# Two schedule entries moved in a fused two-block transformer kernel: linear attention's squares ahead of the third gate, its last two transposes behind one piece

## The chip, the cores and the metric

The kernel runs on one core of a Trainium2 chip. The metric is device time in microseconds (us) for one launch. TensorE does the matrix products, VectorE and ScalarE the elementwise work and the copies out of PSUM, GpSimd one subtraction per piece of weights, SyncE only starts DMAs.

## The reference, cut to what matters

Two layers of a first transformer block are followed by two layers of a second one; batch 1, 256 tokens, width 1024, float32. The change lies in the second block. Its mixer has three branches that are gated, added and projected:

```python
o_nsa = nsa_attention(...)                       # branch 0
o_gla = gated_linear_attention(...)              # branch 1
o_mem = memory_attention(...)                    # branch 2
gates = jax.nn.sigmoid(merge.reshape(B, S, 3, D) + b_merge)
merged = (gates[:, :, 0] * (o_nsa @ w_branch[0]) + gates[:, :, 1] * (o_gla @ w_branch[1])
          + gates[:, :, 2] * (o_mem @ w_branch[2]))
x = x + merged @ w_out
# the end of gated_linear_attention:
o = rms_norm(o, norm_g).reshape(B, S, H * GLA_HEAD_DV)
return o * jax.nn.silu(r)
```

The normalisation of `o` needs, for each token and each of 4 heads, the sum of 128 squares. That is the work whose place is changed, with the transposes that bring the finished branch into the layout that TensorE wants.

## The kernel before, in words

All weights pass through the core once, as 616 pieces of 128 x 1024 floats. SyncE loads a piece into a ring of seven slots (`raw`); ScalarE rounds it to the matmul's format (`round_piece`, L1275, tile `hi`, a ring of five); GpSimd subtracts the rounded part (L542, tile `lo`, in four quarters within the mixers); TensorE multiplies by both parts (L569 to L571, three matmuls for one product: hi by hi, hi by lo, lo by hi) and raises `used`, which frees the slots. ScalarE rounds four pieces ahead (`AHEAD`): the step of a piece on ScalarE rounds the piece four places later in the stream, and needs the `hi` slot that the piece five places before that one has freed.

The order within a mixer is written out by hand. `mix2_work()` says which steps stand behind each piece; `mix2_order()` turns this into one list, and each engine's program walks that list and issues its own part of every step. So an engine's order is fixed, and a step's wait holds up all that the engine has behind it.

At the end of the mixer the order is the four pieces of the memory branch, `rows (2,0)` to `(2,3)`; the four of the NSA branch, `rows (0,0)` to `(0,3)`; two of the linear attention branch, `(1,0)` and `(1,1)`; then `last_branch`, with that branch's other two and the eight of `w_out`. In `last_branch` TensorE takes the first token tile of several pieces before the second tile of any of them. Between them stand:

- `gate b` (ScalarE only, L1631): two sigmoids, 128 x 1024 each. They come behind `(2,0)`, `(2,1)` and `(2,2)`, for branches 2, 0 and 1; `exp_and_ln()` behind the last of them loads the table set of exp and ln (L1264).
- `branch b, m` (VectorE only, L2272 and L2278 or L2282): the product of a branch with its gate, read from PSUM. `rows (0,0)` writes the same banks as the memory branch's, so TensorE waits there for `branch 2, 0` and, before the second token tile, for `branch 2, 1`.
- `gla[3]`: ScalarE waits for `og` (VectorE's copy L2138, the last output of linear attention) and squares eight blocks of 128 columns with a running sum (L1534); VectorE multiplies by the silu of `r` (L2092).
- `gla[4]`: VectorE waits for the sums and takes the variance (L1729). `gla[5]`: ScalarE's `Ln` and `Exp` (L1281, L1282), VectorE's four small steps (L1720 to L1723) and the scaling (L2098), which raises `gscaled`.
- `gla[6]` and `gla[7]`: TensorE waits for `gscaled` and transposes four blocks (L1035) into one bank each; ScalarE takes the rounded part out (`high_part`, L1422, raises `y2hi`), VectorE the rest (L2104, raises `y2lo`). `rows (1,0)` waits for the banks and for `y2lo`.
- `nsa_unit` and `gla_unit`: the last steps of the two attentions, behind `(2,0)` and `(2,1)`.

Of the kernel before, what the change touches and what calls it, by code (L numbers as in the profile page):

```python
# [116 lines left out]
def mix2_work():  # L117

    windows, prep, mem, memory_in, gla, nsa = (
        [(name, i) for i in range(9)] for name in ("windows", "prep", "mem", "memory_in", "gla", "nsa"))  # L120
    cmp = [("cmp", k // 4, k % 4) for k in range(8)]
    mu = [("mem_unit", t) for t in range(6)]
    gu = [[("gla_unit", hp, t) for t in range(5)] for hp in range(2)]
    decay = [[("decay", hp, i) for i in range(4)] for hp in range(2)]
    nu = [("nsa_unit", t) for t in range(NSA_UNITS + 2)]
    none = ()
    return {
        "nk": (none, none, none, none),
        "nq": (none, [memory_in[0]], none, [memory_in[1]]),
        "z3": ([prep[0], windows[0]], [memory_in[2]], [prep[1], windows[1]], [prep[2]]),  # L130
        "mk": (none, [prep[3]], none, [cmp[0], mem[0]]),
        "mq": ([cmp[1], mem[1]], [cmp[2], mem[2]], [cmp[3], mem[3]], [cmp[4], mem[4]]),
        "mv": ([mem[8], cmp[5], mem[5]], [cmp[6], mem[6]], [cmp[7], ("take_cmp",), mem[7]], [mu[0]]),
        "gqk": ([mu[1]], [nsa[0], mu[2]], [mu[3], nsa[1]], [nsa[6], nsa[2]]),
        "gv": ([mu[4], nsa[3]], [gla[0]], [mu[5], nsa[4]], [gla[1], nsa[5]]),
        ("merge", 0): ([gla[2], nu[0]], [decay[0][0]], [nu[1], decay[0][1]], none),
        ("merge", 1): ([nu[2], decay[0][2]], [nu[3]], [decay[0][3]], [nu[4]]),
        ("merge", 2): ([gu[0][0]], [nu[5]], [gu[0][1]], [nu[6], gu[0][2]]),
        ("merge", 3): ([gu[0][3]], [nu[7]], [gu[0][4], decay[1][0]], [nu[8], decay[1][1]]),
        ("merge", 4): ([nu[9], decay[1][2]], [nu[10]], [nu[11], decay[1][3]], [nu[12]]),  # L140
        ("merge", 5): ([gu[1][0]], [nu[13]], [gu[1][1]], [nu[14]]),
        "gr": ([gu[1][2]], [nu[15]], [gu[1][3]], [nu[16]]),
        ("rows", 2): ([nu[17]], [nu[18], gu[1][4]], [gla[3], gla[4]], [gla[5]]),
        ("rows", 0): (none, [gla[6]], [gla[7]], none),
        ("rows", 1): (none, none),
    }


def mix2_order():
    order, merges, work = [], 0, mix2_work()  # L150
    for i, name in enumerate(STRIPS2):
        behind = work[(name, merges) if name == "merge" else name]
        merges += name == "merge"
        for j in range(4):
            order.append(("strip", i, j))
            if j == 3:
                order.append(("take", i))
            order += behind[j]
    for b in BRANCHES:
        for i, steps in enumerate(work["rows", b]):  # L160
            order.append(("rows", b, i))
            if b == 2 and i < 3:
                order.append(("gate", BRANCHES[i]))
            if i == 3:
                order += [("branch", b, m) for m in range(MT)]
            order += steps
    order.append(("last_branch",))
    return order
# [2423 lines left out]
```

## Time and profile before

| | us |
|---|---|
| median of 3 runs (lowest to highest) | 1975.81 (1975.54 to 1976.88) |
| the profiled execution | 1974.96 |
| its span, first to last instruction | 1972.9 |

| engine | busy us | share of the span | instructions |
|---|---|---|---|
| TensorE matmuls (PE) | 1951.8 | 99% | 9698 |
| TensorE weight loads (PEld) | 1578.3 | 80% | 9698 |
| VectorE (DVE) | 719.3 | 36% | 1686 |
| ScalarE (ACT) | 1041.4 | 53% | 1746 |
| GpSimd (POOL) | 1592.1 | 81% | 1160 |

The mean granted clock of TensorE is 0.998 of full speed. The DMA queues moved 348.6 MB, 177 GB/s on average. A share of busy time is an average over stages; what an edit is worth is read where it stands. The second block's two layers have the edited stretch at about 1240 to 1290 us and at 1720 to 1770 us of the span. In the views below, times are microseconds from the start of the span; brackets behind a row give the engine's idle time just before it and what ended it; x4 means four instructions merged into the row.

### The profile page before, as it was taken

Reading aid. Unit: us, or ns where it says so; the run is one execution under the profiler, and the core shown is the slowest. Engines: PE = TensorE matmul, PEld = TensorE weight load, DVE = VectorE, ACT = ScalarE, POOL = GpSimd, SP = SyncE. Lnnn points to the kernel's source line nnn. Section 1 sums busy time; section 2 is a strip of 40 time slices with the busy share of each in tenths; the row PEclk is TensorE's granted clock in tenths of the full one; section 3 lists DMA queues with packets and bytes.
Section 4 is the critical chain, followed back from the end, with each engine's and each line's share of the span. In section 5 each row is a group of like instructions: output and inputs, shape, how many; then the busy total and the mean of one; then the engine's idle time right before and its main releaser. Section 6 shows DMA issues by size and latency. Waiting matters only on the chain.

```text
span 1972.9 us, 26543 instructions
## 1 busy us (share of the span) xinstructions
PE 1951.8 (99%) x9698; PEld 1578.3 (80%) x9698; DVE 719.3 (36%) x1686; ACT 1041.4 (53%) x1746; POOL 1592.1 (81%) x1160
## 2 busy tenths in 40 slices
PE   9999999999999999999999999999999999999999
PEld 7888777888888877788887877778888777778887
DVE  4534444100300354500035677521114577642111
ACT  6445666444644466644466444654446554555443
POOL 7988776988788877598879687878887968788885
PEclk9999999999999999999999999999999999999999
DMA  6655434555565543456565333456557433345553
GB/s 239 233 208 171 161 118 158 184 192 188 206 221 186 178 164 125 139 206 249 186 225 191 119 138 125 153 174 217 211 185 260 150 127 120 129 143 188 183 190 128
DMA packets 98204, 348.63 MB, mean 177 GB/s; under 512 B 13436, under 2 KB 14108, under 8 KB 97820
## 3 DMA queue, kind: packets, MB, share of 16 engines
q1 hardware_dynamic: 97372, 345.80, 49.8%
q8 instruction: 78, 1.28, 0.3%
q10 hardware_dynamic: 704, 1.14, 0.2%
q14 instruction: 50, 0.41, 0.1%
HBM read 345.85 MB, written 1.05 MB: 176 GB/s over the span
## 4 chain that ended last, share of the span: by engine, by line
PE 94%; POOL 2%; ACT 2%; DVE 1%; issue 0%; DMA 0%; SPq 0%; POOLq 0%; ACTq 0%; DVEq 0%
PE psum L569 28%; PE psum L571 27%; PE psum L570 27%; POOL lo L542 2%; PE psum L709 2%; PE psum L752 1%; PE psum L639 1%; PE psum L775 1%; PE psum L762 1%; PE psum L985 1%; PE psum L742 1%; ACT big L1631 1%; ACT hi L1275 0%; PE psum L1139 0%; PE psum L798 0%; PE psum L839 0%
## 5 line engine op out<-in xcount | busy, mean ns | idle before, releaser
L542 POOL TENSOR_TENSOR lo<-raw,hi 128x256 fp32r<-128x256 f32 (+1 forms) x1156 | 1591.9, 1399 | 366.6 <-ACT hi L1275 338.4
L1275 ACT ACTIVATE hi<-raw 128x1024 fp32r<-128x1024 f32 x616 | 646.7, 1059 | 510.7 <-PE psum L571 489.7
L569 PE MATMUL psum<-hi,h_hi 128*128 128x512 f32 x1632 | 651.5, 399 | 2.5 <-POOL lo L542 2.2
L571 PE MATMUL psum<-hi,h_lo 128*128 128x512 f32 x1632 | 637.7, 391 | 0.0
L570 PE MATMUL psum<-lo,h_hi 128*128 128x512 f32 x1632 | 636.5, 390 | 0.0
L569 PEld LDWEIGHTS psum<-hi,h_hi 128*128 128x128 f32 x1632 | 307.3, 188 | 72.4 <-POOL lo L542 6.1
L571 PEld LDWEIGHTS psum<-hi,h_lo 128*128 128x128 f32 x1632 | 306.4, 188 | 65.8
L570 PEld LDWEIGHTS psum<-lo,h_hi 128*128 128x128 f32 x1632 | 307.0, 188 | 60.0
L569 PE MATMUL psum<-hi,y_hi 128*128 128x512 f32 x832 | 333.9, 401 | 4.0 <-DVE big L2272 4.0
L1814 DVE SCALAR_TENSOR_TENSOR big<-psum,small,big 128x256 f32<-128x256 f32 (+1 forms) x120 | 61.1, 551 | 750.4 <-ACT big L1368 750.4
L571 PE MATMUL psum<-hi,y_lo 128*128 128x512 f32 x832 | 325.6, 391 | 0.0
L570 PE MATMUL psum<-lo,y_hi 128*128 128x512 f32 x832 | 325.0, 391 | 0.0
L569 PEld LDWEIGHTS psum<-hi,y_hi 128*128 128x128 f32 x832 | 156.6, 188 | 38.7 <-DVE big L2272 4.9
L571 PEld LDWEIGHTS psum<-hi,y_lo 128*128 128x128 f32 x832 | 156.6, 188 | 33.9
L570 PEld LDWEIGHTS psum<-lo,y_hi 128*128 128x128 f32 x832 | 157.0, 189 | 30.2
L1417 ACT ACTIVATE soft<-soft,small 128x128 f32<-128x128 f32 (+1 forms) x120 | 54.6, 456 | 121.0 <-DVE small L1850 98.3
L1368 ACT ACTIVATE big<-psum,small 128x256 f32<-128x256 f32 (+1 forms) x120 | 57.1, 527 | 83.8 <-PE psum L571 83.7
L1822 DVE TENSOR_TENSOR y_lo<-psum,y_hi 128x512 fp32r<-128x512 f32 (+1 forms) x60 | 49.4, 824 | 38.3 <-ACT y_hi L1377 38.3
L1748 DVE SCALAR_TENSOR_TENSOR h_lo<-psum,special,h_hi 128x128 fp32r<-128x128 f32 x160 | 44.1, 344 | 42.0 <-ACT h_hi L1292 42.0
L1292 ACT ACTIVATE h_hi<-psum,special 128x128 fp32r<-128x128 f32 x160 | 44.5, 379 | 24.6 <-PE psum L639 24.6
L1377 ACT ACTIVATE y_hi<-psum 128x512 fp32r<-128x512 f32 (+1 forms) x60 | 42.8, 713 | 13.1 <-PE psum L709 13.1
L1869 DVE COPY soft<-psum 128x384 f32<-128x384 f32 (+2 forms) x68 | 35.4, 520 | 24.9 <-PE psum L752 24.9
(264 smaller groups left out, 1362.2 us busy)
## 6 DMA issues: line engine op xcount, KB each, us to landing
raw<-in_stream SPq DMA_DIRECT2D x616, 512.0 KB, 3.2
big<-in_w SPq DMA_DIRECT2D x14, 512.0 KB, 7.6
big<-in_post SPq DMA_DIRECT2D x6, 512.0 KB, 4.6
special<-in_b_merge SPq DMA_DIRECT2D x2, 1536.0 KB, 8.1
memkv<-in_mem SPq DMA_DIRECT2D x2, 1024.0 KB, 5.7
big<-in_band SPq DMA_DIRECT2D x2, 768.0 KB, 4.8
x<-in_x SPq DMA_DIRECT2D x2, 512.0 KB, 5.0
special<-in_special SPq DMA_DIRECT2D x2, 512.0 KB, 4.4
```

The costliest lines, as they stand in the source:

```text
L542: t = pool.tensor_tensor(M.lo[:, slot, w], M.raw[:, slot, w], f32(M.hi[:, slot_hi, w]), ALU.subtract)
L569: pe.matmul(out, lhs_hi, rhs_hi, start=start, stop=False)
L570: pe.matmul(out, lhs_hi, rhs_lo, start=False, stop=False)
L571: return pe.matmul(out, lhs_lo, rhs_hi, start=False, stop=stop)
L1275: act.activation(M.hi[:, slot_hi, :], M.raw[:, slot, :], ACT.Copy).then_inc(sem["hi"], 1)
L1292: t = act.activation(out_hi[:, k, toks], psum[:, bank, i * P:i * P + P], ACT.Copy, scale=1.0 if gain is None else gain[:, k:k + 1])
L1368: t = act.activation(act_s[:, m, :], psum[:, bank + m, 0:width], ACT.Silu if gated else ACT.Relu, scale=V.scale[:, m:m + 1])
L1377: act.activation(flat(out), flat(psum[:, bank:bank + kts // 2, :]), ACT.Copy).then_inc(sem["yhi"], 1)
L1417: t = act.activation(out, prob[:, w], ACT.Exp, scale=-1.0, bias=mn[:, i:i + 1], accum_out=total[:, i:i + 1])
L1748: t = dve.scalar_tensor_tensor(out_lo[:, k, toks], psum[:, bank, i * P:i * P + P], gain[:, k:k + 1], f32(out_hi[:, k, toks]), ALU.mult, AL ...
L1814: t = dve.scalar_tensor_tensor(prod_s[:, m, :], psum[:, bank + m, col:col + width], V.scale[:, m:m + 1], act_s[:, m, :], ALU.mult, ALU.mult)
L1822: dve.tensor_tensor(flat(y_lo[:, kt, :]), flat(psum[:, bank:bank + kts // 2, :]), f32(flat(y_hi[:, kt, :])), ALU.subtract).then_inc(sem["y ...
```

## The change

Two steps get another place in the list; nothing is added or taken away, and both layers of the second block have the edit. `gla[3]` moves from behind `rows (2,2)` to behind `rows (2,1)`, and so in front of `gate 1`, the third gate. `gla[6]` moves from behind `rows (0,1)` to behind `rows (0,2)`, where `gla[7]` stands; `(0,2)` is the third piece of the NSA branch (the words that come with the change call it the memory branch's).

```diff
@@ mix2_work()
-        ("rows", 2): ([nu[17]], [nu[18], gu[1][4]], [gla[3], gla[4]], [gla[5]]),
-        ("rows", 0): (none, [gla[6]], [gla[7]], none),
+        ("rows", 2): ([nu[17]], [nu[18], gu[1][4], gla[3]], [gla[4]], [gla[5]]),
+        ("rows", 0): (none, none, [gla[6], gla[7]], none),
         ("rows", 1): (none, none),
```

## Rows read from the trace of the kernel before

**Rows 1.** The page's chain that ended last, shares of the span by engine.

```profile
PE 94%; POOL 2%; ACT 2%; DVE 1%; issue 0%; DMA 0%; SPq 0%; POOLq 0%; ACTq 0%; DVEq 0%
```

**Rows 2.** TensorE's waits: engine line <- releaser: us in total, times, longest.

```profile
PE psum L569 <- DVE big L2272: 4.0, 2, 2.0
...
PE psum L569 <- POOL lo L542: 2.2, 4, 1.3
```

**Rows 3.** Chain of waits, first layer: start us, us, engine and line.

```profile
1247.51 0.36 ACT y_hi L1422
1247.87 0.95 ACT hi L1275
...
1250.74 1.28 ACT L1264
1252.03 0.74 ACT big L1534 x5
...
1254.49 0.95 ACT hi L1275
1255.51 2.84 POOL lo L542 x4
...
1268.37 4.62 POOL lo L542 x4
...
1282.74 3.71 POOL lo L542 x4
```

**Rows 4.** Timeline of VectorE, first layer: start us, us, engine, line, operation, tiles.

```profile
1248.52 0.42 DVE L2138 COPY big<-psum 128x256 f32<-128x256 f32 x1 [0.19 <-PE psum L1002]
...
1254.69 2.35 DVE L2272 TENSOR_TENSOR big<-big,psum 128x1024 f32<-128x1024 f32 x2
...
1259.28 1.72 DVE L2098 TENSOR_TENSOR big<-big,small 128x1024 f32<-128x1024 f32 x1
```

**Rows 5.** Timeline of ScalarE, first layer.

```profile
1255.57 0.21 ACT L1282 ACTIVATE small<-small 128x8 f32<-128x8 f32 x1
...
1262.19 0.69 ACT L1422 ACTIVATE y_hi<-psum,special 128x512 fp32r<-128x512 f32 x1 [2.04 <-PE psum L1035]
```

**Rows 6.** Timeline of TensorE, first layer.

```profile
1252.44 0.39 PE L569 MATMUL psum<-hi,y_hi 128*128 128x512 f32 x1
...
1255.97 0.50 PE L569 MATMUL psum<-hi,y_hi 128*128 128x512 f32 x1 [2.01 <-DVE big L2272]
...
1261.55 0.60 PE L1035 MATMUL psum<-consts,big 128*128 128x128 f32 x4
...
1267.96 0.39 PE L569 MATMUL psum<-hi,y_hi 128*128 128x512 f32 x1
...
1274.76 0.39 PE L569 MATMUL psum<-hi,y_hi 128*128 128x512 f32 x1
...
1286.49 0.50 PE L569 MATMUL psum<-hi,h_hi 128*128 128x512 f32 x1 [1.30 <-POOL lo L542]
```

**Rows 7.** Timeline of TensorE, second layer.

```profile
1735.65 0.73 PE L569 MATMUL psum<-hi,y_hi 128*128 128x512 f32 x1 [2.01 <-DVE big L2272]
...
1739.40 0.39 PE L569 MATMUL psum<-hi,y_hi 128*128 128x512 f32 x1
...
1766.79 0.50 PE L569 MATMUL psum<-hi,h_hi 128*128 128x512 f32 x1 [0.43 <-POOL lo L542]
```

**Rows 8.** Stretch 1736 to 1741: length, busy by engine, then granted clock, DMA share, GB/s.

```profile
1736.00:1741.00 5.00, 5.00 (x16) 3.91 (x16) 4.51 (x6) 1.05 (x2) 4.86 (x6) 0.68 0.06 22
```

**Rows 9.** Timeline of GpSimd, first and second layer.

```profile
1255.51 33.27 POOL L542 TENSOR_TENSOR lo<-raw,hi 128x256 fp32r<-128x256 f32 x37 [2.81 <-ACT hi L1275]
...
1735.19 9.73 POOL L542 TENSOR_TENSOR lo<-raw,hi 128x256 fp32r<-128x256 f32 x12 [2.80 <-ACT hi L1275]
...
1748.39 14.29 POOL L542 TENSOR_TENSOR lo<-raw,hi 128x256 fp32r<-128x256 f32 x16 [0.38 <-ACT hi L1275]
1763.03 6.06 POOL L542 TENSOR_TENSOR lo<-raw,hi 128x256 fp32r<-128x256 f32 x5 [0.35 <-ACT hi L1275]
```

## The prediction

> **What bounds the kernel now.** I read the page's chain first: TensorE holds 94% of it, GpSimd and ScalarE 2% each [rows 1]. So only TensorE's idle time can be won, and there is little of it. The list of its waits has two entries that touch the edited stretch [rows 2]: 4.0 us in two waits on VectorE's L2272 (the memory branch times its gate) and 2.2 us in four waits on GpSimd's L542. Then I read the chain of waits around the first wait on L2272 [rows 3]. The reader is to see that it does not run through that wait. It comes down ScalarE (`y_hi`, rounding, sigmoids, table load, squares, rounding), crosses to GpSimd at 1255.51 and stays there for nine pieces, until TensorE goes on at 1286.49. GpSimd's own timeline says the same: 37 quarter pieces in 33.27 us with no idle time inside [rows 9]. A piece costs GpSimd 2.84 us undisturbed [rows 3], and 0.14 to the next; TensorE takes two and a half from 1267.96 to 1274.76 [rows 6], 2.72 each. GpSimd is the slower of the two here, and the lead it had is used up at the end of the nine. I name pieces by branch and number; the nine are (0,3), (1,0), (1,1), the two of `last_branch` (LB0, LB1) and the first four of `w_out` (E0 to E3).
>
> So TensorE's wait of 2.01 us before (0,0) at 1255.97 is visible but covered: it still stands 1.30 us for E3 [rows 6], and would stand longer if it came sooner. In the second layer the same wait of 2.01 is followed by half clock: the granted clock is 0.68 over 1736 to 1741 [rows 8], so TensorE was at 1.2 GHz for part of it, and a matmul takes 0.73 us instead of 0.39 [rows 7]. From 1735.65 to 1739.40 it does three quarters of a piece, 3.75 us for what takes 3 x 0.68 and about 0.1 for the start: 1.6 us lost. There GpSimd has three short waits for ScalarE's rounding (0.38 and 0.35 are two of them [rows 9]), and TensorE still stands 0.43 us for E3 at 1766.79 [rows 7].
>
> **The change, part by part.** No piece changes its place, so the stream, SyncE's DMAs and their queue, and GpSimd's order are as before. On VectorE nothing moves: `gate` and `rows` issue nothing there, so `gla[3]` to `gla[7]` keep their order among its instructions.
>
> (a) `gla[3]` moves ahead of `rows (2,2)` and of the gate of branch 1. On ScalarE the eight squares now come right behind the `y_hi` of `nsa_unit` 18, ahead of the rounding of (0,2), two sigmoids and the table load. They bring a wait that costs nothing now: `og`, set by VectorE's copy L2138, which ends at 1248.52 + 0.42 = 1248.94 [rows 4]; before, ScalarE comes to it at 1252.03, long after [rows 3]. Now it arrives at 1247.87, the end of `y_hi`, and stands 1.1 us; and 0.1 us of overlap is lost, by which the rounding's start ran ahead of that end. Queued behind the wait on ScalarE are the rounding of (0,2), the sigmoids, the load, and the rounding of (0,3), for which GpSimd waits. These and the squares only swap places, so the rounding of (0,3) ends 1.2 us later, and GpSimd starts on it at 1255.51 + 1.2 = 1256.7. The second layer repeats the first up to this point (2.80 us of GpSimd's idle time ahead of the nine against 2.81 [rows 9]): 1735.19 + 1.2 = 1736.4.
>
> (b) What it buys. The squares take 1254.49 - 1252.03 = 2.46 us [rows 3], so their sums are there at about 1251.5. L2272 is then free to start when the first token tile of (2,3) is done, about 1252.6 (the second tile starts at 1252.44 [rows 6], and the first one's last matmul ends some 0.15 later). One takes 1.2 (2.35 for two [rows 4]), so TensorE may go on at 1253.9, where the second tile is done anyway. The 2.0 us wait goes to 0 to 0.2 in each layer, and with it the cause of the half clock. Taken alone: 2.05 in the first layer, 2.05 + 1.6 in the second, 5.7 in all.
>
> (c) What is late next: GpSimd. The nine pieces take it 1282.74 + 3.71 - 1255.51 = 30.94 us, including the time it is blocked beside VectorE's work (4.62 for LB1 against 2.84) [rows 3]. All of these VectorE steps still fall inside the nine, so I keep 30.94. Their rounding comes in time, since TensorE, being earlier, frees the `hi` slots earlier. First layer: the low part of LB1 is ready at 1268.37 + 4.62 + 1.2 = 1274.2, where TensorE now wants it at 1274.76 - 2.05 = 1272.7: a new wait of 1.5, and 0.55 of the lead is left. Without GpSimd it would be at E3 at 1286.49 - 1.30 - 0.55 = 1284.6; the low part is ready at 1286.45 + 1.2 = 1287.65, so 3.0 more in waits before E2 and E3 together. TensorE passes this point at 1287.7 instead of 1286.49, **+1.2 us**. Second layer: 1736.4 + 30.94 = 1767.35 against 1766.79: **+0.6 us**, since GpSimd's old gaps close. Behind the nine GpSimd waits for TensorE again, so the loss neither grows nor is won back.
>
> (d) `gla[6]` moves behind `rows (0,2)`: four transposes, one `y_hi`, one `y_lo`, as many as before. `gscaled` comes at 1259.28 + 1.72 = 1261.0 [rows 4]; the `Exp` L1282 in front of its chain ends at 1255.78 [rows 5], now 1257.0, where VectorE came to need it before too (L2272 ends at 1254.69 + 2.35). TensorE reaches the old place at 1261.55 - 2.05 = 1259.5 [rows 6] and would stand 1.5 there; behind (0,2) it arrives at 1262.2. Who waits for the moved step: (1,0) needs the banks and `y2lo` of both pairs. With transposes until 1263.1 and two `y_hi` of 0.69 [rows 5], each with a `y_lo` of about that length behind it, they are there by 1265.0, and (1,0) starts at 1267.96 - 2.05 = 1265.9. I cost it at nothing; if that cover of 0.9 fails, GpSimd's nine pieces hide up to 1.5. On ScalarE the rounding of LB0 is now ahead of both `y_hi` and that of LB1 behind both, ready about 1265.2; GpSimd wants it at 1268.37 + 1.2. Nothing.
>
> (e) A table load that the trace doesn't show: `Square` now runs between two pairs of sigmoids, and before it stands behind the load of the exp and ln set. The nearest row is the rounding, a `Copy` between the sigmoids with no load [rows 3]. So 0, or two loads of 1.28 each [rows 3] in front of the rounding of (0,3); a load can't be saved, since no other set is left out. I take 0, as for `Copy`.
> On this the Trainium skill, "ScalarE: Activation LUTs", section "Table sets: the hidden batching unit", says that cheap functions (it names relu, copy, identity and abs) are in every set; it does not name square. Its section "What ACT_TABLE_LOAD costs" puts a switch at 2.66 us with its drain; here a load takes 1.28 and the next instruction starts 0.01 later, so the row decides. By the page's figure two would be an estimated 5.3 us per layer in place of 2.6.
>
> Sum: +1.2 + 0.6 = +1.8 us. The profiled execution took 1974.96 (its span of 1972.9 and 2.1 around it) and would be 1976.8. It lay 0.85 below the median of the runs, 1975.81; on that the forecast is **1977.6**.
>
> **The rivals.**
> *A, the wait was the loss.* GpSimd keeps up and TensorE keeps the 5.7 us: 1970.1. For it: these two waits are the largest in the list [rows 2]. Against: the nine pieces without idle time [rows 9]. It decides by the start of the nine: they would have to begin some 2 us before 1255.5, not after, or take under 28 us.
> *B, table loads.* Two more put the rounding of (0,3) 1.2 + 2.6 = 3.8 us late: +3.8 and +3.2, 1982.8. It decides by whether the sigmoid's set has `Square`.
> *C, the clock, ending slower.* Waits of 1.5 and twice about 1.5 within 14 us take the place of one of 2.0. Of the two waits of 2.01 one was followed by half clock; the one of 1.30 was not. Half clock ahead of E3 costs nothing, since GpSimd sets that point; from E3 on it costs up to 1.6 a layer: 1979.2 with one, 1980.8 with both.
> *D, it doesn't do what it says.* The words that come with the change put the last transposes behind the memory branch's third piece, (2,2); there they would wait for `gscaled` some 10 us. The code puts them behind (0,2), so this has no weight.
>
> **How the numbers follow.** The forecast as in (c): 0.58, 1976.5 to 1978.7. C in one layer 0.14, in both 0.05. A: 0.10. B: 0.08. Faults of the sum (the nine pieces 0.5 shorter or longer in each layer, by how GpSimd's quarters meet VectorE's work; the cover in (d)): 0.05. For 8 in 10 the range holds all but A and B: 1975.0 to 1980.9. A measurement of this kernel tells about 0.2%, 4 us, from no change. Faster by that (below 1971.9) is A and a little of the rest: 0.11. Slower (above 1979.8) is B, C in both layers and a part of C in one: 0.17. Within: 0.72.
>
> **What would show it.** Right: TensorE's waits on L2272 fall from 4.0 to under 0.5 us and those on L542 rise from 2.2 to about 9 to 10, with new ones before LB1 and E2; ScalarE idles 1.1 us before its first square, released by L2138; GpSimd idles before (0,2) and again before (0,3), then works for 31 us without a gap in both layers; the clock stays whole near 1736. Wrong: a rounding of (0,3) that ends before 1255.5; no wait on L542 near 1274; a table load beside L1534 (B); a granted clock under 1 behind E3 (C).

## The result and the profile after

The kernel after takes 1978.42 us (median of 20 runs, 1977.19 to 1979.89) and the kernel before 1975.43 (20 runs, 1974.71 to 1976.88). The ratio is 1.0014 (95%: 1.0008 to 1.0020): 2.8 us slower, 1.6 to 4.0 (the medians are 3.0 apart). The forecast was 1977.6, and 1.8 slower. The profiled executions took 1977.62 and 1974.96, 2.66 apart.

TensorE's waits in the kernel after (engine line <- releaser: us in total, times, longest), against [rows 2]:

```profile
PE psum L569 <- POOL lo L542: 5.3, 5, 2.0
PE psum L1035 <- DVE y_lo L2104: 3.1, 2, 1.6
```

The wait on L2272 is gone from the list. In its place stand 3.1 us more for GpSimd, and an entry that the kernel before does not have at all: the transposes of the linear attention (L1035) wait for VectorE's `y_lo`.

ScalarE's timeline of after, first layer, against [rows 3]:

```profile
1247.42 0.36 ACT L1422 ACTIVATE y_hi<-psum 128x256 fp32r<-128x256 f32 x1
1248.88 0.31 ACT L1534 ACTIVATE big<-big 128x128 f32<-128x128 f32 x1 [1.10 <-DVE big L2138]
...
1251.24 1.05 ACT L1275 ACTIVATE hi<-raw 128x1024 fp32r<-128x1024 f32 x1
1252.19 2.00 ACT L1631 ACTIVATE big<-big 128x1024 f32<-128x1024 f32 x2
1254.20 1.28 ACT L1264 ACT_TABLE_LOAD   x1
1255.50 1.06 ACT L1275 ACTIVATE hi<-raw 128x1024 fp32r<-128x1024 f32 x1
```

The squares come first, after 1.10 us of standing still for the copy L2138. Behind them are the rounding of (0,2), the sigmoids, one table load, and the rounding of (0,3), which ends at 1256.56 where it ended at 1255.44. No load stands beside L1534.

VectorE's timeline of after, first layer, against [rows 4]:

```profile
1252.54 2.58 DVE L2272 TENSOR_TENSOR big<-big,psum 128x1024 f32<-128x1024 f32 x2 [0.93 <-PE psum L571]
```

L2272 now waits for TensorE's products (L571) and no longer for the squares, and starts 2.15 us sooner.

GpSimd's timeline of after, first and second layer, against [rows 9]:

```profile
1252.36 2.84 POOL L542 TENSOR_TENSOR lo<-raw,hi 128x256 fp32r<-128x256 f32 x4 [3.87 <-ACT hi L1275]
1256.64 33.49 POOL L542 TENSOR_TENSOR lo<-raw,hi 128x256 fp32r<-128x256 f32 x37 [1.44 <-ACT hi L1275]
...
1733.97 2.85 POOL L542 TENSOR_TENSOR lo<-raw,hi 128x256 fp32r<-128x256 f32 x4 [3.87 <-ACT hi L1275]
1738.24 33.56 POOL L542 TENSOR_TENSOR lo<-raw,hi 128x256 fp32r<-128x256 f32 x37 [1.43 <-ACT hi L1275]
```

It stands before (0,2), stands again before (0,3), and then works through 37 instructions. These are the 36 quarters of the nine pieces and one whole piece behind them (2.38 us), which the view counts in with the quarters. The nine pieces start 1.1 us later on the clock of the trace (1256.64 against 1255.51), and they set the end.

TensorE's timeline of after, against [rows 6] and [rows 7]:

```profile
1264.29 0.33 PE L1035 MATMUL psum<-consts,big 128*128 128x128 f32 x1 [1.56 <-DVE y_lo L2104]
...
1284.91 0.63 PE L569 MATMUL psum<-hi,h_hi 128*128 128x512 f32 x1 [1.99 <-POOL lo L542]
...
1288.18 0.65 PE L569 MATMUL psum<-hi,h_hi 128*128 128x512 f32 x1
...
1290.17 0.48 PE L569 MATMUL psum<-hi,h_hi 128*128 128x512 f32 x1
...
1766.56 0.50 PE L569 MATMUL psum<-hi,h_hi 128*128 128x512 f32 x1 [2.00 <-POOL lo L542]
...
1769.51 0.50 PE L569 MATMUL psum<-hi,h_hi 128*128 128x512 f32 x1 [0.85 <-POOL lo L542]
```

The waits are before E2 (1.99 and 2.00) and E3. In the first layer TensorE comes to E3 late instead of waiting for it, because half clock follows the wait for E2. Two stretches of after, 1284 to 1289 and 1736 to 1741 (columns as in [rows 8]):

```profile
1284.00:1289.00 5.00, 4.09 (x13) 3.31 (x14) 0.66 (x2) 0.86 (x4) 4.86 (x6) 0.66 0.01 3
1736.00:1741.00 5.00, 5.00 (x23) 4.06 (x22) 3.08 (x5) 4.37 (x6) 3.57 (x6) 1.00 0.64 197
```

So near 1736, where the kernel before had 0.68, the clock is whole. The half clock (1.2 GHz) has gone to the first layer.

The account of the 2.66: TensorE comes to this stretch 0.1 us earlier than in the trace of before. It passes E3's second token tile at 1290.17, against this row of before:

```profile
1288.36 0.48 PE L569 MATMUL psum<-hi,h_hi 128*128 128x512 f32 x1
```

That makes 1.8 + 0.1 = 1.9 lost in the first layer. In the second it passes E3 at 1769.51 against 1766.79, 2.7, of which 1.8 was brought along: 0.9 lost there. Behind E3 the two traces run in step.

### The profile page after: what moved, and what is told of

Same layout as the page of the kernel before. It is cut to its first block, busy times and chain, and to the rows that moved or that the text cites. A ratio compares the mean times of both kernels' runs of the same rounds, so it can differ in the third digit from the quotient of the medians.

```text
span 1975.6 us, 26543 instructions
## 1 busy us (share of the span) xinstructions
PE 1952.4 (99%) x9698; PEld 1578.5 (80%) x9698; DVE 718.8 (36%) x1686; ACT 1043.0 (53%) x1746; POOL 1591.9 (81%) x1160
## 3 DMA queue, kind: packets, MB, share of 16 engines
q8 instruction: 78, 1.28, 0.3%
HBM read 345.85 MB, written 1.05 MB: 176 GB/s over the span
## 4 chain that ended last, share of the span: by engine, by line
PE 94%; POOL 4%; ACT 1%; DVE 0%; issue 0%; DMA 0%; SPq 0%; POOLq 0%; DVEq 0%; ACTq 0%
PE psum L569 28%; PE psum L571 27%; PE psum L570 27%; POOL lo L542 4%; PE psum L709 2%; PE psum L752 1%; PE psum L639 1%; PE psum L762 1%; PE psum L775 1%; PE psum L985 1%; PE psum L742 1%; PE psum L1139 0%; PE psum L839 0%; PE psum L798 0%; PE psum L941 0%; PE psum L953 0%
## 5 line engine op out<-in xcount | busy, mean ns | idle before, releaser
L542 POOL TENSOR_TENSOR lo<-raw,hi 128x256 fp32r<-128x256 f32 (+1 forms) x1156 | 1591.7, 1400 | 369.5 <-ACT hi L1275 340.7
L571 PE MATMUL psum<-hi,h_lo 128*128 128x512 f32 x1632 | 638.2, 391 | 0.0
L571 PEld LDWEIGHTS psum<-hi,h_lo 128*128 128x128 f32 x1632 | 306.7, 188 | 65.6
L571 PE MATMUL psum<-hi,y_lo 128*128 128x512 f32 x832 | 325.0, 391 | 0.0
L571 PEld LDWEIGHTS psum<-hi,y_lo 128*128 128x128 f32 x832 | 156.1, 188 | 33.9
```

What stands on the lines that cost most here:

```text
L542: t = pool.tensor_tensor(M.lo[:, slot, w], M.raw[:, slot, w], f32(M.hi[:, slot_hi, w]), ALU.subtract)
L571: return pe.matmul(out, lhs_lo, rhs_hi, start=False, stop=stop)
```

## The experiments

The theory (T): GpSimd's nine pieces set the end of the stretch, so what counts is when (0,3) is rounded, and the squares ahead of it delay that. The main rival (R): the loss comes from somewhere else, from the new wait of the moved transposes or from the clock. Each kernel was timed in 5 rounds beside the kernel before on the same chip, whose median was 1975.5 to 1975.8 each time. Ratios are to it, with the 95% interval; differences in us come from the ratio or from the medians, which differ by up to 0.6 us. A piece's rounding has the number of its piece, although `round_piece` is called `AHEAD` steps before.

### One half of the change at a time

e1 is the kernel before with `gla[3]` moved alone, e2 with `gla[6]` moved alone.

```diff
-        ("rows", 2): ([nu[17]], [nu[18], gu[1][4]], [gla[3], gla[4]], [gla[5]]),
+        ("rows", 2): ([nu[17]], [nu[18], gu[1][4], gla[3]], [gla[4]], [gla[5]]),
```
```diff
-        ("rows", 0): (none, [gla[6]], [gla[7]], none),
+        ("rows", 0): (none, none, [gla[6], gla[7]], none),
```

> Only the squares move; the two transposes stay where they were. Theory (GpSimd's nine pieces, started by the rounding of (0,3), set the point E3): the rounding is as late as in the changed kernel, so the time is that of the changed kernel, +2.7 us on the kernel before, although TensorE now waits 1.6 us a layer for gscaled in front of the first transposes. Rival (the time is lost in TensorE's new wait at the last transposes, 1.57 us a layer behind (0,2)): that wait is gone, and what comes in its place decides; if waiting for gscaled is as dear the two can't be told apart here.

> Only the first pair of transposes moves, the squares stay behind the third gate. TensorE gets the wait of 1.57 us a layer for the first pair's low part. Theory: GpSimd's nine pieces start and end as before; the wait uses up TensorE's old waits for E3 (1.30 and 0.43 us), so the time is 0.3 + 1.1 = +1.4 us. Rival (the wait at the transposes counts in full): +3.1 us. Rival (only the squares matter): 0.

The squares alone: 1978.85 us, 1.0016 (1.0007 to 1.0025), as slow as both together. The transposes alone: 1978.31, 1.0012 (1.0003 to 1.0021). TensorE's waits of e1, and after them those of e2:

```profile
PE psum L569 <- POOL lo L542: 4.5, 4, 2.0
...
PE psum L1035 <- DVE big L2098: 2.4, 2, 1.2
```
```profile
PE psum L569 <- DVE big L2272: 4.0, 2, 2.0
PE psum L1035 <- DVE y_lo L2104: 3.1, 2, 1.6
```

In e1 the transposes wait 1.2 us for `gscaled` at their old place, and it costs nothing beyond what after has. So the squares alone are enough for the whole loss of the change. In e2 the wait for L2272 stays as it was, and the transposes' wait comes on top. The 2.4 us (0.6 to 4.1) lie between what T and R gave, so the time alone decides nothing between them. The runs of e2 also fall into two groups, five at 1976.0 to 1976.5 and six at 1978.3 and above. The trace says more. GpSimd's timeline of e2, first layer:

```profile
1284.48 6.06 POOL L542 TENSOR_TENSOR lo<-raw,hi 128x256 fp32r<-128x256 f32 x5 [0.36 <-ACT hi L1275]
```

GpSimd has caught up and stands 0.36 us just before E3, for ScalarE's rounding; so GpSimd doesn't set E3 here. With the later start of its trace taken off, TensorE passes E3 0.75 us later than in before in the first layer and 1.7 in the second. In the first layer 0.9 of the 1.57 were covered by the wait for E3 (1.30 before, 0.40 here), in the second nothing was (0.43 in both). T had put 0.3 and 1.1 there. The halves don't add up: 3.1 + 2.4 would be 5.5 where both together cost 2.8.

### Does the moved transposes' wait cost anything in the kernel after?

`gla[7]` waits until both output banks are read out, so behind (0,2) it waits for the `y_lo` of the pair just before it. e6 is the kernel after in which each pair waits for its own bank.

```diff
-                wait_free(0)
-                wait_free(1)
+                wait_free(pair)
```

> The changed kernel, in which the second pair of last transposes waits for its own bank alone and no longer for the first pair's. TensorE's wait of 1.57 us a layer there goes. Theory: GpSimd still sets E2 and E3, its nine pieces start as late, so the time stays within 0.5 us of the changed kernel (+2.3 to +3 on the kernel before) and TensorE's waits for GpSimd grow by the 3.1 us. Rival (the wait at the transposes is what the change costs): 3.1 us less than the changed kernel, -0.3 on the kernel before.

1978.2 us, 1.0013 (1.0004 to 1.0021): as the kernel after. TensorE's waits of e6, and then its timeline, first layer:

```profile
PE psum L569 <- POOL lo L542: 6.9, 6, 2.0
```
```profile
1274.47 0.51 PE L569 MATMUL psum<-hi,y_hi 128*128 128x512 f32 x1 [1.23 <-POOL lo L542]
```

The entry on L1035 is gone, and the time is given back further down: a wait of 1.23 us before LB1 appears, the one that the prediction had priced at 1.5. R falls: the 1.57 us a layer are idle time that GpSimd hides.

### Is it the date of (0,3)'s rounding?

e3 keeps the squares ahead of the gate, but rounds (0,2) before them and (0,3) before the sigmoids.

```diff
             elif i == 3:
+                round_piece(piece["rows", 2, 2] + AHEAD)
                 act.wait_ge(sem["og"], 4 * layer + 4)
...
             elif what == "gate":
                 b = step[1]
+                if b == 1:
+                    round_piece(piece["rows", 2, 3] + AHEAD)
```

> The changed kernel, with ScalarE's rounding of (0,2) put ahead of its wait for og and the rounding of (0,3) put right behind the squares, ahead of the third gate. Nothing else moves. Theory: GpSimd starts the nine pieces at 1252.7 instead of 1256.6, E3's low part is there by 1283.9, and TensorE comes at 1284.9 with its waits for the memory branch's product and the half clock gone: -1.6 in the first layer, -2.1 in the second, -3.7 us on the kernel before, 6.4 below the changed kernel. Rival (the new wait at the transposes or the clock is what the change costs): within 1 us of the changed kernel, +1.7 to +3.7.

1972.32 us, 0.9984 (0.9975 to 0.9992): 3.2 faster than before and 6 faster than after, with the squares where the change put them. GpSimd's timeline of e3, first layer (its trace runs 1.6 us later than that of before at this point; over 8 to 16 us, at the start of the kernel, its granted clock is 0.57 and that of before 0.79):

```profile
1250.52 6.78 POOL L542 TENSOR_TENSOR lo<-raw,hi 128x256 fp32r<-128x256 f32 x8 [0.29 <-ACT hi L1275]
1258.72 24.03 POOL L542 TENSOR_TENSOR lo<-raw,hi 128x256 fp32r<-128x256 f32 x28 [1.41 <-ACT hi L1275]
```

(0,2) and (0,3) now follow each other without idle time. The gap of 1.41 is before (1,0), whose rounding has become the late one.

e4b turns the same knob the other way: the kernel before, with four unused copies on ScalarE in front of the rounding of (0,3).

```diff
             elif what == "rows":
+                if step == ("rows", 2, 3):
+                    for _ in range(4):
+                        own(act.activation(V.gla_prod[:, 1024:1280], M.x[:, 0, 0:256], ACT.Copy))
                 round_piece(piece[step] + AHEAD)
```

> The kernel before, with four extra ScalarE copies of 128 x 256 (results not used, about 1.7 us together) in front of the rounding of (0,3); the squares and TensorE's waits up to (0,0) are untouched. Theory: GpSimd's nine pieces start 1.7 us later, +1.7 in the first layer and +1.1 to +1.7 in the second: about +3 us, all of it in TensorE's waits for GpSimd near E2 and E3, with the two waits of 2.0 for the memory branch's product as before. Rival (that product's wait is what bounds this stretch): 0.

1979.68 us, 1.0018 (1.0009 to 1.0027): 3.6 slower. Timeline of e4b, ScalarE and then GpSimd, and its waits of TensorE:

```profile
1254.83 1.74 ACT L1626 ACTIVATE big<-x 128x256 f32<-128x256 f32 x4
1256.60 1.06 ACT L1275 ACTIVATE hi<-raw 128x1024 fp32r<-128x1024 f32 x1
```
```profile
1257.74 33.46 POOL L542 TENSOR_TENSOR lo<-raw,hi 128x256 fp32r<-128x256 f32 x37 [4.59 <-ACT hi L1275]
```
```profile
PE psum L569 <- POOL lo L542: 6.1, 6, 2.0
PE psum L569 <- DVE big L2275: 4.0, 2, 2.0
```

The copies take 1.74 us. The wait for the memory branch's product (here L2275) is untouched, and the waits for GpSimd rise from 2.2 to 6.1. A delay of the rounding, without any squares, makes the loss. The granted clock is whole in both layers behind the waits of 2.0 (1.00 over 1285 to 1290 and over 1767 to 1772), and that execution took 1978.63, 3.7 more than the profiled one of before; so half clock isn't needed for the loss. (An earlier form with two copies of 128 x 1024 has a race between the copies and the squares and gave no time.)

### Is an early rounding enough without the squares?

e10 is the kernel before with (0,3) rounded right behind the sigmoids, ahead of the table load and of the squares.

```diff
                 if b == 1:
+                    round_piece(piece["rows", 2, 3] + AHEAD)
+                if b == 1:
                     exp_and_ln()
```

> The kernel before with one edit: the rounding of (0,3) right behind the third gate's sigmoids, ahead of the table load and the squares; squares and transposes as in the kernel before. GpSimd starts the nine pieces 3 us sooner, but the squares end 1.3 us later (0.3 for the slot of (2,2), 1.0 for the rounding), and with them VectorE's product and (0,0). Theory: TensorE's wait at (0,0) grows from 2.0 to 3.3, its waits for GpSimd at E3 (1.30 and 0.43) go, and what bounds is TensorE: -0.05 in the first layer, +0.9 in the second, 0 to +1 in all, more if half clock follows the longer waits. Rival (GpSimd alone counts): -1.7 or better.

1979.42 us, 1.0019 (1.0010 to 1.0028): 3.8 slower, a miss for both. The squares now end later, and L2272 with them. TensorE's waits of e10 (L2274 is L2272 there):

```profile
PE psum L569 <- DVE big L2274: 7.4, 2, 3.7
```

3.7 us a layer, and half clock behind it in both layers. GpSimd's timeline of e10, first layer:

```profile
1286.00 6.06 POOL L542 TENSOR_TENSOR lo<-raw,hi 128x256 fp32r<-128x256 f32 x5 [0.35 <-ACT hi L1275]
```

Here too GpSimd stands 0.35 us before E3, in both layers, and TensorE's own pace sets the end. Counted from where each trace comes to the wait for L2272, TensorE passes E3 2.3 us later than in before in the first layer and 1.7 in the second, 4.0 in all. The 1.7 are the longer wait in full (3.68 against 2.01); the half clock stood in that layer of before as well. In the first layer the half clock is new too, and 0.9 of both is covered (the wait for E3 was 1.30 and is 0.43). So GpSimd covers the wait for L2272 only as long as it is itself the later one. Squares first and roundings first are both needed; either alone loses.

### Both together: a version that beats both kernels

e8 is e3 with the pair's own bank (the edit of e6) and with (1,0) rounded ahead of the table load too.

```diff
                 if b == 1:
+                    round_piece(piece["rows", 0, 0] + AHEAD)
+                if b == 1:
                     exp_and_ln()
```

> e3_round_first with two more edits: the rounding of (1,0) stands behind the third gate's sigmoids, ahead of the table load, and the second pair of last transposes waits for its own bank alone. In e3_round_first GpSimd stood idle 1.4 us between (0,3) and (1,0), still ended last at E3 (waits of 0.5 and 0.4 us), and TensorE lost 1.57 us a layer at the transposes. Theory: E3 is ready 1.3 us sooner and TensorE is there 1.6 sooner: 1.2 to 1.6 us less in each layer than e3_round_first, -5.7 us on the kernel before. Rival (something else than GpSimd's pieces sets the pace): no better than e3_round_first, -3.3.

1970.12 us, 0.9971 (0.9960 to 0.9982): 5.4 faster than the kernel before by the medians and 8.3 faster than the kernel after. GpSimd's timeline of e8 and then its waits of TensorE:

```profile
1249.18 37.48 POOL L542 TENSOR_TENSOR lo<-raw,hi 128x256 fp32r<-128x256 f32 x41 [0.31 <-ACT hi L1274]
```
```profile
PE psum L569 <- POOL lo L542: 2.5, 4, 1.1
```

One run from (0,2) on, the 40 quarters of ten pieces and one whole piece; neither of the two gaps is left. What remains of waiting is about 1.05 for E3 in each layer. (e8 has 7 runs, 1969.88 to 1970.56.)

e5 leaves (1,0)'s rounding out of e8, and e11 leaves the own bank out of it.

> e8_three_rounded without its early rounding of (1,0): the roundings of (0,2) and (0,3) early, and the second pair of transposes waiting for its own bank alone. Theory: TensorE comes to E3 1.57 us sooner than in e3_round_first, but GpSimd's pieces from (1,0) on start as late as there, and e3_round_first waited for them already; so the time is that of e3_round_first (-3.4 on the kernel before) within 0.6 us. Rival (the transposes' wait is what is left): 3.1 us less, -6.5.

> e8_three_rounded with TensorE's wait for the first pair's low part put back. In e8_three_rounded TensorE stood 1.0 us for E3 in each layer, and the wait put back is 1.57. Theory: the first 1.0 of it is covered, so 0.5 to 0.6 us a layer slower than e8_three_rounded, -4.4 on the kernel before. Rival (each wait counts in full): 3.1 slower than e8_three_rounded, -2.4.

e5: 1972.36 us, 0.9983 (0.9974 to 0.9992), as e3: the rounding of (1,0) is worth 2.2. e11: 1972.32, 0.9985 (0.9976 to 0.9994), 2.2 slower than e8, between what the two theories gave. The chain of waits of e11, first layer, shows what E3 waits for there (its start, with L639, is as in the chain of before that stands further down):

```profile
1280.33 0.46 ACT h_hi L1292 x2
1280.79 0.95 ACT hi L1275
1281.81 3.73 POOL lo L542 x4
1285.58 0.50 PE psum L569
```

GpSimd is idle for 0.36 us before E3, since E3's rounding stands on ScalarE behind the `h_hi` of TensorE's own transposes (L639). From the transposes to E3 it is a loop of TensorE itself, and whatever delays TensorE ahead of it delays the end one for one. So the idle time that GpSimd hid in after and e6 (1.57 us a layer) costs here, since GpSimd is no longer late: 2.2 of 3.1. The theory had covered 1.0 a layer by e8's wait for E3; but 0.43 of such a wait is part of the loop, and counted from the copy that sets `og`, E3 comes 1.2 us later in e11 in the first layer and 1.1 in the second.

### Whole pieces for E0 to E3

A whole piece takes GpSimd 2.40 us, four quarters take 2.84 and 0.14 to the next piece. e7b is the kernel after with E0 to E3 whole.

```diff
-    return 8 <= at < PIECES2 - 8 * MLP_STRIPS - 4
+    return 8 <= at < PIECES2 - 8 * MLP_STRIPS - 8
```

> The changed kernel, in which GpSimd subtracts the first four pieces of w_out (E0 to E3) whole and not in quarters: a whole piece takes 2.40 us elsewhere, four quarters 2.84 and more with VectorE beside them. The start of the nine pieces is as late as in the changed kernel. Theory: E3 is ready some 3 us sooner, so TensorE's waits for E2 and E3 (2.0 and 2.9 us) mostly go: -2 to -3.5 in each layer, to between -1 and -3.5 us on the kernel before, if VectorE's own operations, blocked longer by a whole piece, don't hold TensorE. Rival (the transposes' wait or the clock is the cost): as the changed kernel, +2.7.

1979.71 us, 1.0022 (1.0013 to 1.0031): 4.2 slower than before where T had a gain, a miss. Waits of TensorE in e7b, and then its timeline of VectorE:

```profile
PE psum L639 <- DVE big L2282: 7.5, 7, 2.0
```
```profile
1277.65 4.92 DVE L2282 TENSOR_TENSOR big<-big 128x512 f32<-128x512 f32 x2
```

TensorE hardly waits for GpSimd any more (0.5 us in all), but up to 2.0 us for VectorE's L2282. Two of these take 4.92 here; in the kernel after, where GpSimd works in quarters, the same two take 1.84 and the next two 2.32. Both inputs of L2282 are in SBUF. L2272, with one in PSUM, keeps its 1.22 in both kernels. The Trainium skill, "SBUF — State Buffer", section "Who interferes with whom", says that a VectorE instruction with two SBUF inputs contends with a GpSimd instruction that reads SBUF, and that this contention is an exclusive lock. The trace agrees: the two L2282 end at 1279.82 and 1282.57, each 0.55 us behind the end of a whole piece on GpSimd (1279.27 and 1282.02), and the 2.6 to 3.1 us more are about one whole piece of 2.40. The quarters cost GpSimd time and give VectorE its turn.

### The kernel after once more

> The changed kernel once more, beside the others on the same chip: +2.8 us on the kernel before, 6 to 8 above e8_three_rounded.

1979.02 us, 1.0017 (1.0008 to 1.0026), as in the result. In its profile the half clock is in both layers; the stretches behind E2's wait:

```profile
1284.00:1289.00 5.00, 2.98 (x12) 1.86 (x10) 1.65 (x2) 0.40 (x2) 4.86 (x6) 0.86 0.00 1
...
1766.00:1771.00 5.00, 3.02 (x11) 2.21 (x10) 1.56 (x2) 0.00 (x0) 4.86 (x6) 0.79 0.00 0
```

The same kernel, with the same waits of 2.0, had it in one layer in the first profile and in both in this one. Rival C is a matter of the execution.

## Why the prediction was right

*What bounds the kernel.* Right for the first layer; for the second see below. The waits' list named L2272 first with 4.0 us, and taking it away won nothing, because in the first layer the chain of waits did not run through it, and in the second GpSimd's nine pieces were close behind. e3 and e4b moved the nine pieces alone, one way and the other, and the time followed.

*(a) and (b).* Right. ScalarE stood 1.10 us for L2138 (1.1 forecast), (0,3) was rounded 1.2 us late with the 0.1 by which the trace runs ahead, and the wait on L2272 went to nothing.

*(c) The nine pieces.* Right in kind, a little small. The 37 quarters in 33.27 us are 36 quarters and a whole piece; the sum took the nine pieces from the chain and is not touched by it. They took 1287.80 - 1256.64 = 31.16 us in the first layer and 31.2 in the second where 30.94 was put down: +0.2 each. In the first layer TensorE started E3 0.4 after its low part was ready, and lost 0.1 more on its first token tile, at half clock: that is C in one layer, to which 0.14 was given. So +1.2 became +1.9: 1.2 + 0.2 + 0.5. In the second layer +0.6 became +0.9.

*(d) The transposes.* Wrong in the mechanism, right in the price. I had TensorE pass them until 1263.1 without a wait, and overlooked that `gla[7]` waits for both banks, the first of which the first pair has just filled: 1.56 us at 1264.29. This wait takes the place of the forecast one before LB1 (1.5), and so L542's waits came to 5.3 and not to 9 to 10; 5.3 + 3.1 = 8.4 is the idle time that the forecast meant. It cost nothing, because GpSimd's nine pieces hid it, the cover that the prediction named for another fault; e6 shows it. That a whole wait of 1.56 could be overlooked without harm is luck of this kernel: in e2 and e11, where GpSimd is on time, the same wait costs 2.4 and 2.2 us.

*The second layer of before.* Wrong, without harm to the sum. I read TensorE's 0.43 us for E3 as GpSimd's lateness. The chain of waits of before, second layer, has:

```profile
1734.38 1.23 DVE big L2272
1735.65 0.73 PE psum L569
...
1760.29 0.23 PE psum L639 x2
1760.54 0.93 ACT h_hi L1292 x5
1761.56 0.46 ACT h_hi L1292 x2
1762.01 0.95 ACT hi L1275
1763.03 3.72 POOL lo L542 x4
1766.79 0.50 PE psum L569
```

GpSimd had caught up and waited 0.35 us for that rounding [rows 9]: the same loop of TensorE as in e11. So in this layer the chain does run through the wait for L2272, and the reading of one chain, the first layer's, missed it. But little of the 3.65 us that (b) puts on the wait and its half clock could be won. GpSimd's idle time within its nine pieces is 0.27 + 0.38 + 0.35 = 1.0 us, and with that gone the nine would set E3. The change did remove the wait and the half clock, and the delayed nine came out 0.9 behind all the same.

*(e) The table.* Right, and B falls: the squares run behind the sigmoids with no load, and a load takes 1.28 us.

*The rivals.* A asked for nine pieces that begin 2 us sooner. They begin later, and it falls; e3 and e8 bring them forward, and get 3.2 and 5.4 us of its 5.7. C happened in one layer of the profiled execution, for 0.5 us, and in both of another. D fell with the code. The forecast has no half clock in it and the measured time has some, and its range held that time by 0.3 us.

## What to carry to other kernels

The largest wait in a list is not worth its length: follow the chain, and see whether another engine's run without idle time ends at the same point. On an engine that works in order, pulling a step forward pulls its wait forward too, and everything behind it pays. Ask which of those is on the chain, here a rounding that feeds GpSimd, and put that one first. Then the same move gains 3.2 us (e3) instead of costing 2.8, and 5.4 with one more rounding ahead and the pair's own bank (e8). Look at the chain in every layer: here the first and the second differed.

## What was unexpected of the hardware

A wait of TensorE of 2.0 us was followed by a granted clock under 1 in some executions and not in others. Before had it behind one of its two, and so had e2; after behind one of two and in the second profile behind both; e1 and e6 behind both; e7b behind one of two; e4b behind none of its four. In e3, e5, e8 and e11, whose waits in this stretch are at most 1.6, no half clock was seen; behind e10's 3.7 it was seen both times. What decides it at 2.0 stays open.
